# Reordering the last stores of a gated-attention stage, and taking two store buffers out of a wait list

## The reference

```python
h = jnp.einsum('bsd,de->bse', x, w_in)
q, k, v, g, a_low, u, z, gate_a, gate_b = jnp.split(h, SPLIT_POINTS, axis=-1)
...
o = gla_chunked(q, k, v, log_a)                       # state carried over chunks of the sequence
y_a = rms_norm_heads(o, gn_w) * jax.nn.silu(g)
p = causal_multiscale_pool(u.reshape(B, S, POOL_GROUPS, POOL_GROUP_DIM))
p = jnp.einsum('bsgc,gcd->bsgd', p, pool_w).reshape(B, S, POOL_WIDTH) + pool_b
y_b = p * pool_scale * jax.nn.silu(z)
merged = jax.nn.sigmoid(gate_a) * (y_a @ w_a) + jax.nn.sigmoid(gate_b) * (y_b @ w_b)
return layer_norm(DEEPNORM_ALPHA * x + merged @ w_o, ln_w, ln_b)
```

## Time and profile before

| | |
|---|---|
| runs shown | median 595.69 us of 3 (595.4 to 597.3) |
| the profiled execution | 592.98 us, of which its slowest core's span is 591.3 us |
| spans of the 8 cores | 586.8 to 591.3 us; core 6 is the slowest |
| PE busy | 567.0 us, 96% of the span |
| DVE busy | 440.2 us, 74% |
| ACT busy | 282.4 us, 48% |
| POOL busy | 86.7 us, 15% |
| PE on the chain that ended last | 86% |

### The profile page before, as it was taken

How to read it: one execution, slowest core, us unless ns; L and a number is a source line. 1 busy time by engine, 2 the same in 40 slices (tenths; PEclk the granted TensorE clock), 3 DMA queues, 4 the chain that set the end, 5 groups by cost and what they waited for, 6 DMA issues and landing times.

```text
span 591.3 us, 10077 instructions; the slowest of 8 cores (586.8 to 591.3 us)
## 1 busy us (share of the span) xinstructions
PE 567.0 (96%) x2886; PEld 275.5 (47%) x2942; DVE 440.2 (74%) x860; ACT 282.4 (48%) x598; POOL 86.7 (15%) x152
## 2 busy tenths in 40 slices
PE   6999999999999998899999999999999989999994
PEld 2344445555555653344444444444444434455553
DVE  2478998888777793888877878456775519988896
ACT  2479965656665674344332333666633212223223
POOL 1110004444544350000001000100000001000010
PEclk9999999999999999799999999999999999999998
DMA  8999933177492618705115303895500054454442
GB/s 229 321 176 171 163 64 99 46 109 134 61 144 61 88 50 116 99 0 73 19 19 60 48 1 39 134 161 96 72 1 1 1 177 143 142 184 143 147 170 108
DMA packets 48006, 60.19 MB, mean 102 GB/s; under 512 B 30864, under 2 KB 36624, under 8 KB 45648
## 3 DMA queue, kind: packets, MB, share of 16 engines
q0 software_dynamic: 7184, 21.50, 24.5%
q1 hardware_dynamic: 36304, 33.97, 22.6%
q10 hardware_dynamic: 4464, 4.08, 2.8%
HBM read 61.10 MB, written 14.16 MB: 127 GB/s over the span
## 4 chain that ended last, share of the span: by engine, by line
PE 86%; DMA 6%; DVE 3%; SPq 2%; issue 2%; ACT 1%; DVEq 0%; ACTq 0%
PE pb L950 24%; PE pb L1044 14%; PE pb L679 9%; PE pb L712 8%; PE pb L1528 8%; PE pb L409 5%; PE pb L1480 4%; PE pb L1488 3%; PE pb L429 3%; DMA yscr<-A 2%; DMA A<-head 2%; DMA A<-x 1%; PE pb L1512 1%; SPq L306 1%; PE pb L769 1%
## 5 line engine op out<-in xcount | busy, mean ns | idle before, releaser
L1044 PE MATMUL pb<-A,ws 128*128 128x512 bf16 x251 | 63.3, 379 | 0.3
L679 PE MATMUL pb<-A,xT 128*128 128x512 bf16 x249 | 61.4, 379 | 0.5
L1543 ACT ACTIVATE junk<-xT 128x512 bf16<-128x512 f32 (+1 forms) x33 | 20.2, 612 | 80.8 <-DVE xT L1537 80.6
L950 PE MATMUL pb<-A,ws 128*128 128x512 bf16 x212 | 52.8, 379 | 0.2
L950 PE MATMUL pb<-xT,ws 128*128 128x512 bf16 x169 | 44.4, 386 | 2.8 <-DVE ws L869 2.6
L955 ACT COPY sgm_t<-pb 128x512 f32<-128x512 f32 x54 | 31.6, 585 | 31.9 <-PE pb L950 31.7
L804 POOL TENSOR_SCALAR A<-A,eblast 128x256 bf16<-128x256 f32 x30 | 29.7, 990 | 65.6 <-ACT A L805 36.9
L1044 PEld LDWEIGHTS pb<-A,ws 128*128 128x128 bf16 x256 | 25.0, 98 | 30.2
L1021 ACT ACTIVATE sgm_t<-sgm_t 128x512 f32<-128x512 f32 x24 | 15.1, 630 | 47.5 <-DVE sgm_t L981 24.2
L679 PEld LDWEIGHTS pb<-A,xT 128*128 128x128 bf16 x256 | 24.9, 98 | 24.6 <-issue 0.8
L950 PE MATMUL pb<-A 128*128 128x512 bf16 x133 | 35.5, 387 | 0.6 <-ACT pb L961 0.4
(11 more groups left out here) (182 smaller groups left out, 1158.0 us busy)
## 6 DMA issues: line engine op xcount, KB each, us to landing
ws<-wts POOLq DMA_DIRECT2D x10, 1024.0 KB, 11.1
A<-head SPq DMA_DIRECT2D x32, 256.0 KB, 10.0
A<-x SPq DMA_DIRECT2D x16, 512.0 KB, 4.3
out<-xT SPq DMA_DIRECT2D x15, 512.0 KB, 2.9
A<-wts POOLq DMA_DIRECT2D x7, 1024.0 KB, 27.1
yscr<-A ACTq DMA_DIRECT2D x29, 128.0 KB, 2.7
kscr<-A SPq DMA_DIRECT2D x12, 128.0 KB, 2.0
xT<-xt POOLq DMA_DIRECT2D x2, 512.0 KB, 11.0
```

The lines of the kernel that those rows point to most:

```text
L679: PE(lambda e, k=k: e.matmul(pb[bank][:, :], xTc(c, k), W.ap[:, k, :], start=(k == 0), stop=(k == KC - 1)), r=[W.b], w=[bb[bank]])
L950: PE(lambda e, k=k: e.matmul(pb[bank][:, :], u(k), x(k), start=first and k == 0, stop=k == 3, skip_group_check=True), r=[ub] + xb, w=[bb[b ...
L1044: PE(lambda e, k=k: e.matmul(pb[bank][:, :], W.ap[:, k, m * 128:(m + 1) * 128], aT[:, k, tb * 512:(tb + 1) * 512], start=(k == 0), stop=(k ...
```

## The change

`st_Y` gets an argument that selects its store, its transposes or both. After the loop over the steps the stores of n = 29, 30 and 31 are issued first, and the transposes of n = 30 and n = 31 behind them. The list that goes into `free_g` has only the first two of the four store buffers.

```diff
-        def st_Y(n):
+        def st_Y(n, part=(0, 1)):
...
-            P.add("sp" if n > 28 else "act", lambda e: e.dma_start(
-                out=yscr[tb, hp, (c % 4) * 128:(c % 4 + 1) * 128, :], in_=yb_s[n % 4].rearrange("p j f -> p (j f)")),
-                reads=[b_ybs[n % 4]], writes=[b_ysc[tb][c % 4][hp]], lane=f"ys{n % 4}")
-            if c % 4 == 3:
+            if 0 in part:
+                P.add("sp" if n > 28 else "act", lambda e: e.dma_start(
+                    out=yscr[tb, hp, (c % 4) * 128:(c % 4 + 1) * 128, :], in_=yb_s[n % 4].rearrange("p j f -> p (j f)")),
+                    reads=[b_ybs[n % 4]], writes=[b_ysc[tb][c % 4][hp]], lane=f"ys{n % 4}")
+            if c % 4 == 3 and 1 in part:
...
-        gla_bufs = [b for k in b_vg for r in k for b in r] + b_kds + b_sTs + b_ybs + b_Sbf[0] + b_Sbf[1] + b_S + b_junk
+        gla_bufs = [b for k in b_vg for r in k for b in r] + b_kds + b_sTs + b_ybs[0:2] + b_Sbf[0] + b_Sbf[1] + b_S + b_junk
...
         for n in (NS - 2, NS - 1):
             st_y(n)
-            st_Y(n - 1)
-        st_Y(NS - 1)
+            st_Y(n - 1, (0,))
+        st_Y(NS - 1, (0,))
+        for n in (NS - 2, NS - 1):
+            st_Y(n, (1,))
```

## The result

The change ran in 590.3 us (median of 4 runs) against 596.08 us for the kernel before in the runs made with it: ratio 0.9896, 95% interval 0.9872 to 0.992. The ratios in this document are formed from the single runs, so they differ a little from those of the medians, and they leave out two runs in which one die ran at a lower granted clock (632.71 us of the change, 624.02 us of the list alone). The forecast of 588.8 us beside 595.69 us is a ratio of 0.9884. In later runs beside other kernels the change gave 0.9906, 0.9885 to 0.9928. The gain is about 1% by both, some 6 us of the 6.87 us forecast; the forecast lies inside the first interval and at the low end of the second, just outside it.

What follows compares the result with a forecast made beforehand. PE, busy 96% of the span, bounds the kernel; time is lost where it waits or runs at lower clock. Loss 6.96 less new wait 0.09 gives 6.87 us off 595.69: 588.8 us, range 587.2 to 592.0 us.

Steps and rivals of the forecast that it cites:

- 6.87 us forecast: Whole gain on core 6: 6.96 us of loss removed less a new wait of 0.09 us; chance 0.80.
- The loss of 6.96 us: Start of the u quads: groups of products 1 and 5 13.00 us apart instead of 6.04, from waits and lower clock.
- The slowest core: Core 6 would stay slowest at 584.4 us, core 3 at 582.9 us, so the whole gain counts.
- The list or the order: First sum's wait: the shorter list alone removes it; the earlier store and transposes gain nothing by themselves.
- The landing of the store: Store of n = 31, issued ahead of the weight load: taken to land in 1.91 us, between 1.91 and 11.00 us.
- The new wait of 0.09 us: PE's product 4 after the old stall: due at 241.51 us, could start at 241.60 us; bounds 0 and 0.7 us.
- only the waiting comes back: Rival at the old stall: the clock falls for another reason, only 4.1 us return, 591.6 us; chance 0.08.
- the wait changes its name: Rival at the first sum: something else in its list ends at about 235 us, time stays 595.7 us; chance 0.07.
- The slower one: Rival: transposes delay the gate_a weight load; harm from 18.3 us after issue, gain gone at 25.2 us; chance 0.05.
- The ports: Gate_a weight load: busy DVE in two-port mode could delay its start; sum unchanged unless the delay passed the 6.9 us slack.

Runs made afterwards that it cites:

- the list alone: Kernel before with only the shorter wait list, stores and transposes in the old order: 587.86 us, ratio 0.9883 to the kernel before.
- the third experiment: Kernel before with neither part of the change, the weight load just ahead of the store of n = 31 issued later: 587.72 us, ratio 0.9907.
- the order alone: The change with the old, full wait list, only the order of stores and transposes new: 587.74 us, ratio 0.9884 to the kernel before.
- the first of the two late loads: The change with the load of the gate_a weights moved 8.7 us later among PE's groups: 588.36 us, ratio 0.9896 to the kernel before.

## Why the prediction was right

The measured 590.3 us lies inside the forecast range of 587.2 to 592.0 us, and the path by which it was to come is the one that the runs show.

*The loss of 6.96 us* was the right thing to read: one distance that takes in both waits and the slow clock. The distance fell back to 6.05 us, and the time from there to the end fell by 6.4 us in the mean of the cores, 6.07 us in the runs beside each other and 5.8 us in the first. The few tenths between 6.4 and the stalls' mean of 6.8 us, and between both and the medians, are within the intervals; I can't say where they went.

*The slowest core.* The sum took the loss of core 6, because core 6 would stay the slowest; in the profiled execution core 3 was. That this did no harm is luck: the loss of core 6 lies near the mean of the cores, 6.8 us, while single cores lost 5.5 to 7.8 us. The 7.6 us of core 3, which the prediction calls an extreme, is not the largest: core 5 of the kernel before lost 13.87 - 6.04 = 7.8 us.

*The list or the order.* The prediction said that the shorter list alone removes the wait, and of the order that it "gains nothing by itself". The first was right. The second was wrong as it was put: on top of the list the order gains nothing, but without the list it makes the whole gain, since the store lands at about 220 us.

*The landing of the store* was taken as 1.91 us between bounds of 1.91 and 11.00 us; it is 1.7 us, a little below the lower bound. The reason given, that it comes ahead of the weight load, is what the third experiment shows.

*The new wait of 0.09 us* is there in size (6.13 - 6.04), on all eight cores, but not for the reason given; that the size agrees is luck. The prediction held that DVE's 6.17 us of work between L981 and the next L975 would be too long. That counts to the recorded end of the scan which comes last in it, 244.64 + 1.28 = 245.92 us in the kernel before:

```profile
244.64 1.28 DVE L1122 TENSOR_TENSOR_SCAN wg_s<-A,pfix 128x512 bf16<-128x512 bf16 x1
```

When nothing holds L976 up, it starts 1.20 us behind the start of that scan (238.79 and 239.99 us in the order alone), 0.08 us ahead of its recorded end. The same work then takes 239.99 - 233.90 = 6.09 us, and the distances are 6.04 to 6.05 us: it just fits. In the change DVE stands 0.31 us ahead of L976, which puts L982 6.14 us behind the one before it (236.63 - 230.49) in place of 6.05 us (233.90 - 227.85), and that 0.09 us goes through.

*The rivals.* That only the waiting comes back is refuted by the granted clock of 1.00 from 230 us on. That the wait changes its name is refuted by the list of waits. The slower one was rightly placed. Harm to DVE was put at a landing 18.3 us after the old issue time: on core 7 of the first of the two late loads it landed 8.7 + 10.6 = 19.3 us after it, and DVE waited 0.9 us, which cost PE nothing. The whole gain was to be gone at 25.2 us: the cores where the load landed 25.1 to 25.3 us after that time lost 7.1 to 7.4 us. Between the two, charging each us of lateness as one of time is a balance of two things that the prediction left out. The lead of DVE over PE takes something off, so that three cores lost only 3.1 to 3.3 of 4.4 to 4.6 us, and the lower clock puts 1.9 to 2.2 us on where it comes.

*The ports.* The load issued with DVE at work (236.98 us on core 6) landed in 9.7 us, against 10.2 us with DVE idle before (issued at 234.46 us). So the late start that the prediction took from the Trainium skill (SBUF — State Buffer, "Who interferes with whom") shows in no row of this kernel; whether DVE was in a two-port mode at that moment no row shows either, so the rule is not tested.

## What to carry to other kernels

When a wait list is built from whole groups of buffers, compare it with the addresses that are really overwritten: here two buffers that those sums never wrote over brought in a store that landed 11 us after its issue. Read the price of a stall as the lengthening of a distance that otherwise repeats exactly, since it holds the second wait and the slow clock that the waits alone (4.1 of 7.0 us) don't show. And issue a small DMA that something waits for ahead of a large load, even one from another queue: here that made 1.7 us of 10 to 12 us.

## What was not expected of the hardware

A store of 128 KB that was issued 0.6 us behind a load of 1024 KB on another queue took 10 to 12 us to land, within 0.4 us of the load's own time on each core of the kernel before; with four transposes ahead of it and no load it took 1.9 to 2.8 us.

What the lower clock costs grows far less than the waiting before it: 2.0 to 3.8 us for 3.5 to 12.0 us of PE's waiting at the old place, 1.9 to 2.2 us for 2.9 to 5.2 us at the gate_a load. And waits of nearly one length ended both ways there: behind 2.9 to 3.0 us the granted clock stayed at 1.00 on three cores and fell to 0.50 on a fourth (2.92 us).

In the kernels with the short list DVE stands 0.31 us ahead of L976 for nothing that the profile shows, and the third distance is 6.12 to 6.16 us on all eight cores; in the two kernels that keep four lanes in that list and don't stall, the distances are 6.04 to 6.05 us. The instructions differ by two waits on semaphores. What the 0.31 us is stays open; it is too little to show in the time.
